# Down projections of four feed-forward stages: eight block products before, seven after

## What is computed

```python
def swiglu(h, w_gu, w_down):
    gate, up = jnp.split(h @ w_gu, 2, axis=-1)
    return (jax.nn.silu(gate) * up) @ w_down      # (256 x 2816) @ (2816 x 1024)

def sublayer(x, shift, scale, gate, g_pre, g_post, fn, res_weight):
    h = rmsnorm(x, g_pre) * (1 + scale[:, None, :]) + shift[:, None, :]
    return x + res_weight * gate[:, None, :] * rmsnorm(fn(h), g_post)
```

## Time and profile before

| | us |
|---|---|
| median of three timed runs | 2773.78 |
| lowest and highest of them | 2773.39 and 2774.01 |
| span of the profiled execution | 2775.9 |
| gate/up products of stage 0, 20 of 22 units | 138.41 |
| down products of one stage | 75.80 |
| the tail, from 1400 us to the end | 1376 |

### The profile page before, as it was taken

How to read it: one execution, slowest core, us unless ns; L and a number is a source line. 1 busy time by engine, 2 the same in 40 slices (tenths; PEclk the granted TensorE clock), 3 DMA queues, 4 the chain that set the end, 5 groups by cost and what they waited for, 6 DMA issues and landing times.

```text
span 2775.9 us, 26672 instructions
## 1 busy us (share of the span) xinstructions
PE 2463.2 (89%) x9819; PEld 1566.6 (56%) x9819; DVE 1601.6 (58%) x3550; ACT 620.1 (22%) x1778; POOL 685.0 (25%) x698
## 2 busy tenths in 40 slices
PE   7999999999999999999998877967988778877776
PEld 6874558856884678758654432634535535432222
DVE  4552144524451545513697885686887877874445
ACT  2001210001000220000143333342333533332222
POOL 1110001100110001100243443444444443444332
PEclk9999999999999999999999999989999989999999
DMA  9994427954894339957799999999999999999997
GB/s 382 383 372 165 152 95 271 361 231 152 319 363 170 144 149 380 370 202 269 293 376 421 421 422 421 413 412 421 415 421 400 421 421 415 421 392 422 421 422 326
DMA packets 120520, 931.58 MB, mean 336 GB/s; under 512 B 15133, under 2 KB 16565, under 8 KB 20422
## 3 DMA queue, kind: packets, MB, share of 16 engines
q0 software_dynamic: 94032, 670.65, 59.1%
q1 hardware_dynamic: 26358, 259.23, 23.7%
HBM read 928.74 MB, written 1.09 MB: 335 GB/s over the span
## 4 chain that ended last, share of the span: by engine, by line
PE 58%; DMA 27%; DVE 8%; ACT 3%; issue 2%; SPq 1%; POOL 1%; DVEq 0%
DMA ring<-in_peer_uv_dram,lamt 26%; PE psR L975 20%; PE psF L893 11%; PE psF L1325 10%; DVE ring L2567 3%; PE psR L863 2%; PE psR L833 2%; PE psR L822 2%; PE psR L1350 1%; POOL ring L679 1%; PE psR L1422 1%; PE psF L921 1%; PE psR L874 1%; ACT small L1765 1%; PE psF L1192 1%
## 5 line engine op out<-in xcount | busy, mean ns | idle before, releaser
L1325 PE MATMUL psF<-ring,p_diag 128*128 128x512 f32 x1792 | 868.2, 629 | 248.0 <-ACT p_diag L1771 247.7
L679 POOL DMA_INDIRECT ring<-in_peer_uv_dram,lamt x512 | 592.8, 1158 | 984.3 <-PE psF L1325 757.9
L2567 DVE SCALAR_TENSOR_TENSOR ring<-ring,h 128x1024 f32<-128x1024 f32 x512 | 620.9, 1223 | 345.5 <-DMA ring<-in_peer_uv_dram,lamt 342.4
L1325 PEld LDWEIGHTS psF<-ring,p_diag 128*128 128x128 f32 x1792 | 337.0, 198 | 709.3 <-ACT p_diag L1771 369.4
L975 PE MATMUL psR<-hT,ring 128*128 128x256 f32 x2560 | 553.3, 379 | 0.6 <-DMA ring<-in_gu_t_dram 0.6
L975 PEld LDWEIGHTS psR<-hT,ring 128*128 128x128 f32 x2560 | 486.2, 190 | 66.5 <-DMA ring<-in_gu_t_dram 0.7
L893 PE MATMUL psF<-ring,arena 128*128 128x512 f32 x704 | 303.2, 593 | 4.0 <-DVE arena L2207 4.0
L1762 ACT ACTIVATE small<-small 128x2 f32<-128x2 f32 x255 | 51.8, 203 | 825.6 <-DVE ring L2567 825.4
L893 PEld LDWEIGHTS psF<-ring,arena 128*128 128x128 f32 x704 | 133.5, 190 | 172.0 <-issue 166.4
L509 POOL DMA_DIRECT2D mring<-in_mod_t_dram x80 | 42.5, 531 | 746.3 <-DVE mring L2032 742.2
L2207 DVE TENSOR_TENSOR arena<-arena,psR 128x256 f32<-128x256 f32 x80 | 33.7, 421 | 249.7 <-ACT arena L1632 249.6
(11 more groups left out here) (341 smaller groups left out, 2289.3 us busy)
## 6 DMA issues: line engine op xcount, KB each, us to landing
ring<-in_gu_t_dram SPq DMA_DIRECT2D x44, 2048.0 KB, 9.0
mring<-in_mod_t_dram POOLq DMA_DIRECT2D x80, 1024.0 KB, 7.8
M<-in_mod_t_dram POOLq DMA_DIRECT2D x40, 1024.0 KB, 8.1
ring<-in_down_t_dram SPq DMA_DIRECT2D x20, 2048.0 KB, 9.3
mring<-in_tail_w_dram SPq DMA_DIRECT2D x40, 1024.0 KB, 9.3
ring<-in_conv_in_t_dram SPq DMA_DIRECT2D x12, 2048.0 KB, 8.1
ring<-in_gla_in_t_dram SPq DMA_DIRECT2D x6, 2048.0 KB, 7.7
ring<-in_out_t_dram SPq DMA_DIRECT2D x6, 2048.0 KB, 7.7
```

The lines of the kernel that those rows point to most:

```text
L679: pool.indirect_dma_start(out=pair(n % PAIRS), out_offset=None, in_=rows, in_offset=bass.IndirectOffsetOnAxis(ap=s_idx[:, c:c + 1], axis=0 ...
L1325: ins = pe.matmul(psF[:, b, f * HALF:(f + 1) * HALF], p_diag[:, n % PAIRS, :], row_v(n % PAIRS)[:, f * HALF:(f + 1) * HALF], start=(i == 0 ...
L2567: dve.scalar_tensor_tensor(row_u(c), row_u(c), 1.0, h[:, b, :], ALU.mult, ALU.mult, accum_out=p_dots[:, c:c + 1]).then_inc(dot_done, 1)
```

## The change

The down projection is taken as a 2 x 2 by 2 x 2 product of blocks, once for each pair p of neighbouring tiles (k = 2p, 2p + 1; eleven pairs). The left blocks are two tiles of actT by two token blocks, the right ones two weight tiles by two column halves. Instead of eight products a pair takes seven (the Strassen form with shared sums), each with a PSUM bank of its own, accumulated over all pairs.

- VectorE makes for each pair four sums of activation blocks, 128 x 128 (sum_acts), after every second gate/up unit, and four sums of weight blocks, 128 x 512 (sum_weights): pair 0 after unit 20's half steps, pair 1 after the last unit's, the others after that. The three weight sums that get their own room are double-buffered in h and hT; the sum for pair p waits for product 4 of pair p - 2 (weights_sums_used). The fourth is written over the weight tile itself.
- TensorE waits for both kinds of sum ahead of each pair (sums_ready), and no longer for the last unit before the first product. Pairs 0 to 4 take all seven products. Pairs 5 to 10 leave out products 2 and 3 (LATE_PAIRS); pairs 9 and 10 run product by product, in the order 1, 6, 7, 5, 4; then come products 2 and 3 of the six late pairs, 12 products.
- VectorE joins the seven banks into psF with eight additions or copies of 512 columns. Five can be made before product 4 is complete and one follows it (sum_products); the result for b = 0 is then whole, and ScalarE waits for that (down_summed) instead of output_done. One more, for product 2, stands between finish and prepare of b = 0, and the last, for product 3, after TensorE's last product and in front of store_modulated (sum_second).
- The stage's left-over half steps are interleaved, one behind each sum_weights; tables() stands between sum_weights 1 and 2 in stage 0.
- Down weights are stored in another order of tiles (DOWN_ORDER). Two of the preloaded chunks move one and two places later in SP's queue, because sums of activations now lie in their room.

```diff
@@ -74,9 +74,14 @@
 TURN_UNIT = (12, 15, 16, 17)
 BLOCK_KEYS_UNIT, BLOCK_SCORE_UNIT = 22, (25, 28, 31, 34)
 KEPT = {6: 5, 3: 6, 9: 7, 0: 4, 11: 8, 18: 3}
-PRELOADED = (3, 6, 9)
+PRELOADED = (6, 3, 9)
 PASSING = [(b, c) for b in range(2) for c in range(CHUNKS) if c not in KEPT]
 
+
+PAIRED = FT // 2
+LATE_PAIRS = range(5, PAIRED)
+DOWN_ORDER = [k for p in range(5) for k in (2 * p, 2 * p + 1)] + [2 * p for p in LATE_PAIRS] + [2 * p + 1 for p in LATE_PAIRS]
+ACT_SUMS = (7552, 10752, 10752, 8704)
 
 SHARED_GROUPS = range(4, 36)
...
@@ -202,7 +207,11 @@
     cb = view(6144, KD, P)
 
     actT = view(0, FT, T)
+    h_flat, hT_flat = h[:].rearrange("p b n -> p (b n)"), hT[:].rearrange("p k t -> p (k t)")
+    weight_sums = [v[:, 0:3 * HALF].rearrange("p (m n) -> p m n", m=3) for v in (h_flat, hT_flat)]
     sg = view(FT * T, 2, T)
+    sum_p1, sum_p16, sum_p167, sum_p165 = arena[:, FT * T:FT * T + HALF], hT_flat[:, 0:HALF], hT_flat[:, HALF:2 * HALF], \
+        h_flat[:, 3 * HALF:]
 
     knT = view(6144, MH, T)
     vmla = view(8192, TB, D)
...
@@ -480,6 +495,25 @@
             return psF[:, 1, (u % 3) * HALF:(u % 3 + 1) * HALF]
         return psW[u % 3][:]
 
+    def act_sum(which, m, p):
+
+        q = m * PAIRED + p
+        return arena[:, ACT_SUMS[which] + q * P:][:, 0:P] if q < 30 else macc[:, 0, (q - 30) * P:(q - 29) * P]
+
+    def down_tile(st, k):
+
+        q = DOWN_ORDER.index(k)
+        return slot(st.w + 11 + q // 4, 4, D)[:, q % 4, :]
+
+    def down_slot(k):
+        return DOWN_ORDER.index(k) // 4
+
+    def product_bank(st, product):
+
+        if product in (6, 7):
+            return psW[(st.u + 17 + product) % 3]
+        return {1: psM[:], 4: psF[:, 0, 0:HALF], 5: psF[:, 0, HALF:], 2: psF[:, 1, 0:HALF], 3: psF[:, 1, HALF:]}[product]
+
     def output_done(eng, st, b):
 
         if b == 0:
...
@@ -611,8 +645,10 @@
             load_chunk(first_chunk(n)[0], n)
 
         def load_kept(c):
-            if c in PRELOADED:
+            if c == PRELOADED[0]:
                 sp.wait_ge(x_ready, x_count(6))
+            elif c in PRELOADED:
+                sp.wait_ge(w_used, outputs[ffn3.w + LOADS["ffn"] - 1])
             elif KEPT[c] < 4:
                 sp.wait_ge(a_full, LAST_QUERY[KEPT[c] + 4] + 1)
             else:
...
@@ -639,8 +675,8 @@
                     sp.wait_ge(m_used, 2 * len(PIECES) + 2)
                     for n in range(2):
                         load_first(n)
-                if st is conv7 and j in (2, 3, 4):
-                    load_kept(PRELOADED[j - 2])
+                if st is conv7 and j in (2, 4, 5):
+                    load_kept(PRELOADED[(2, 4, 5).index(j)])
                 fill(st.w + j)
 
         for n in range(2, FIRST_CHUNKS):
...
@@ -883,33 +919,48 @@
                 u = block_by_tokens(u, w, lhs, kd, n, b)
             return u
 
-        def project(st, i, lhs, kt):
-
-            tail = 4 * ((kt - 1) // 4 - 1)
-
-            def rows_of(k, b):
-                w = slot(i + k // 4, 4, D)
-                for f in range(2):
-                    ins = pe.matmul(psF[:, b, f * HALF:(f + 1) * HALF], lhs[:, k, b * P:(b + 1) * P],
-                                    w[:, k % 4, f * HALF:(f + 1) * HALF], start=(k == 0), stop=(k == kt - 1))
-                return ins
-
-            for k in range(tail):
-                if k % 4 == 0:
-                    arrived(i + k // 4)
-                for b in range(TB):
-                    ins = rows_of(k, b)
-                if k % 4 == 3:
+        def down(st):
+
+            def product(m, p):
+
+                k, kk = 2 * p, 2 * p + 1
+                w, ww, sums = down_tile(st, k), down_tile(st, kk), weight_sums[p % 2]
+                lhs, rhs = {1: (actT[:, k, P:], w[:, 0:HALF]), 2: (actT[:, kk, P:], ww[:, 0:HALF]),
+                            3: (act_sum(st.which, 2, p), ww[:, HALF:]), 4: (actT[:, kk, 0:P], sums[:, 2, :]),
+                            5: (act_sum(st.which, 0, p), w[:, HALF:]), 6: (act_sum(st.which, 1, p), sums[:, 0, :]),
+                            7: (actT[:, k, 0:P], sums[:, 1, :])}[m]
+                return pe.matmul(product_bank(st, m), lhs, rhs, start=(p == 0), stop=(p == PAIRED - 1))
+
+            def sums_ready(p):
+                pe.wait_ge(act_summed, PAIRED * st.which + p + 1)
+                pe.wait_ge(weights_summed, PAIRED * st.which + p + 1)
+
+            for p in range(PAIRED - 2):
+                sums_ready(p)
+                for m in (1, 6, 7, 5):
+                    ins = product(m, p)
+                if p == 6:
                     ins.then_inc(w_used, 1)
-            for b in range(TB):
-                for k in range(tail, kt):
-                    if b == 0 and k % 4 == 0:
-                        arrived(i + k // 4)
-                    ins = rows_of(k, b)
-                    if b == 0 and k == kt - 1:
-                        ins.then_inc(first_ready, 1)
-                    if b == 1 and (k % 4 == 3 or k == kt - 1):
+                product(4, p).then_inc(weights_sums_used, 1)
+                if p not in LATE_PAIRS:
+                    for m in (2, 3):
+                        ins = product(m, p)
+                    if p in (1, 3):
                         ins.then_inc(w_used, 1)
+            for m in (1, 6, 7, 5, 4):
+                for p in (PAIRED - 2, PAIRED - 1):
+                    if m == 1:
+                        sums_ready(p)
+                    ins = product(m, p)
+                    if m == 4 and p == PAIRED - 2:
+                        ins.then_inc(w_used, 1)
+                ins.then_inc(first_ready if m == 4 else product_done, 1)
+            for m in (2, 3):
+                for p in LATE_PAIRS:
+                    ins = product(m, p)
+                    if m == 3 and p == 8:
+                        ins.then_inc(w_used, 1)
+                ins.then_inc(product_done if m == 2 else w_used, 1)
 
         def project_block(i, lhs, b):
...
@@ -977,8 +1028,8 @@
                                             start=(k == 0), stop=(k == KD - 1))
                     ins.then_inc(unit_full, 1)
                     u += 1
-            have(u - 1)
-            project(st, st.w + 11, actT, FT)
+            have(u - 2)
+            down(st)
 
         def gla(st):
             i = st.w
...
@@ -1983,7 +2034,10 @@
 
             for b in range(1 if st.kind == "mla" else 0, TB):
                 if st.kind not in ("kv", "conv"):
-                    output_done(act, st, b)
+                    if st.kind == "ffn":
+                        act.wait_ge(down_summed, TB * st.which + b + 1)
+                    else:
+                        output_done(act, st, b)
                     root_mean_square(st, psF[:, b, :], b)
                 if st.n < 6:
                     x_roots(stages[st.n + 1], b)
...
@@ -2206,10 +2260,79 @@
                 dve.wait_ge(gate_ready, t_gate.next())
                 dve.tensor_tensor(actT[:, j, :], sg[:, j % 2, :], ps[:, T:2 * T], ALU.mult).then_inc(unit_stored, 1)
                 u += 1
+                if j % 2 == 0:
+                    dve.wait_ge(unit_stored, u - 1)
+                    sum_acts(st, j // 2 - 1)
                 for _ in range(halves_done(st, j) - halves_done(st, j - 1)):
                     half_step()
-            while halves_taken.n < sum(2 * len(BESIDE[n]) for n in BESIDE if n <= st.n):
-                half_step()
+                if j == FT - 2:
+                    sum_weights(st, 0)
+            dve.wait_ge(unit_stored, u)
+            sum_acts(st, PAIRED - 1)
+            sum_weights(st, 1)
+            if st.n == 0:
+                tables()
+            for p in range(2, PAIRED):
+                sum_weights(st, p)
+                if halves_taken.n < sum(2 * len(BESIDE[n]) for n in BESIDE if n <= st.n):
+                    half_step()
+            sum_products(st)
+
+        def sum_acts(st, p):
+
+            k, kk = 2 * p, 2 * p + 1
+            b0, b1 = [[actT[:, t, b * P:(b + 1) * P] for t in (k, kk)] for b in range(TB)]
+            s1, s2, s4 = [act_sum(st.which, m, p) for m in range(3)]
+            link(dve.tensor_tensor(s1, b0[0], b0[1], ALU.add))
+            dve.tensor_tensor(b0[0], b1[0], b0[0], ALU.subtract)
+            link(dve.tensor_tensor(s2, s1, b1[0], ALU.subtract))
+            dve.tensor_tensor(s4, b1[1], s2, ALU.subtract).then_inc(act_summed, 1)
+
+        def sum_weights(st, p):
+
+            k, kk = 2 * p, 2 * p + 1
+            w, ww = down_tile(st, k), down_tile(st, kk)
+            if p >= 2:
+                dve.wait_ge(weights_sums_used, (PAIRED - 2) * st.which + p - 1)
+            for i in sorted({down_slot(k), down_slot(kk)}):
+                dve.wait_ge(w_loaded[home_of(st.w + 11 + i)], landed[st.w + 11 + i])
+            t2, t3, t4 = [weight_sums[p % 2][:, m, :] for m in range(3)]
+            b11, b12, b21, b22 = w[:, 0:HALF], w[:, HALF:], ww[:, 0:HALF], ww[:, HALF:]
+            dve.tensor_tensor(t3, b22, b12, ALU.subtract)
```

(48 more changed lines are left out.)

## The result

| | before | after |
|---|---|---|
| median of the runs, us | 2773.90 (4 runs) | 2755.82 (4 runs) |
| lowest and highest | 2773.39 and 2778.68 | 2749.45 and 2755.93 |
| span of the profiled execution | 2775.9 | 2747.7 |

The ratio is 0.9924, with a 95% interval from 0.991 to 0.9938: 18.1 us less in the medians. The profiled execution is the one of 2749.45 us; the three others lie within 0.2 us of 2755.8. That gap of 6.4 us is the main thing to explain, since the forecast was 2750.8. Wherever both are given, the device time stands 1.7 to 1.8 us above the span. So the profiled execution of the kernel before took some 2777.7 us, an estimate, and was 3.8 us longer than the median, where its span alone shows 2.0.

What follows compares the result with a forecast made beforehand. TensorE was taken to bound the stages that change. Products saved less gaps, clock and boundaries leave 6.8 us each in stages 2, 4, 6 and 2.6 in stage 0: 2773.8 - 23.0 = 2750.8 us, range 2745 to 2761.

Steps and rivals of the forecast that it cites:

- rival A: Down projections: the clock also falls at the four gaps of 2.16 us, 6.8 us, giving 2757.6; chance 0.12.
- Rival B: TensorE's many short gaps in the four stages together lower its clock; about 2773 us, no change; chance 0.05.
- Rival D: The front ends earlier but the tail, with its full DMA, ends when it did; 2773.8 us; chance 0.04.
- gap behind the tables: Stage 0: tables() between weight sums 1 and 2 takes 5.8 us and leaves TensorE 2.5 us idle.
- gap at pair 8: Stage 0: weight sum 8 is ready at 48.1 us but wanted at 47.0, so TensorE idles 1.1 us.
- gap ahead of pair 10: Each down projection: sum_weights 10 waits for product 4 of pair 8, so TensorE idles 2.16 us.
- Products: Down projections: seven products instead of eight per pair, 0.861 us each, save 9.5 us per stage, 37.9 us in all.
- Prices of sums: VectorE: sum_weights 2.76 us and sum_acts 1.16 us per pair; PSUM sums at SBUF's price, or 0.75 us as other end.
- Boundary: End of each stage: the 12-product cover for b = 0 holds, L2086 starts later; 0.2 us lost per stage.
- Moved DMA loads, half steps: Later preloaded chunks and loads costed at nothing; no half step's DMA wait over a microsecond in the down projections.
- Rival C: Down projections: half steps' DMA waits now stand in front of TensorE, 73 us slower, 2823 us; chance 0.04.
- Clock: Half clock only behind stage 0's 2.5 us gap, 1.7 us with 0.6 left; the 2.16 us gaps at full clock.

Runs made afterwards that it cites:

- e1: The changed kernel run again without any edit: median 2757.59 us in six runs, ratio 0.9926 to the kernel before.
- e3: Changed kernel with TensorE starting each pair on products that need no weight sum, reading tiles as loaded: 2736.64 us, ratio 0.9855 to the kernel before.
- e7: Kernel before with only the two preloaded chunks moved later in SyncE's queue: 2775.74 us, ratio 1.0.
- e5: Changed kernel with one useless VectorE sum more in front of sum_weights 10 in each stage: 2759.45 us, ratio 0.9936 to the kernel before.
- e6: Changed kernel with the weight buffer given back one product earlier (order 6, 7, 1, 4, 5): 2747.64 us, ratio 0.9898 to the kernel before.
- e2: Changed kernel with the weight buffer given back two products earlier (order 6, 7, 4, 1, 5): 2743.65 us, ratio 0.9882 to the kernel before.
- e4: e3 with VectorE's stage 0 work reordered, tables() behind weight sum 2 and left-over half steps later: 2732.80 us, ratio 0.9845 to the kernel before.

## Why the prediction was right, and where it was not

The forecast was 2750.8 us in a range from 2745 to 2761. Measured were 2755.8 and, with six more runs, 2757.6 us. Inside the range, right in sign and size, but the usual time is that of rival A (2757.6), which had a chance of 0.12, and the forecast's own is the rarer one: 2749.45 and 2750.88, two runs of ten.

That the forecast's 23.0 us meets the 23.4 us between the first two profiles is in part luck: 1.6 us of these are the GLA stage's clock, and the fall that was priced at 0.6 us in stage 0 did not come there, while one that wasn't counted cost 1.7 us in stage 6. With the clock left out on both sides, 23.0 + 0.6 = 23.6 us stand against 21.8 + 1.7 = 23.5 us. So the products, the idle gaps and the boundaries were right by more than luck, and the clock was not. The chances don't quite fit each other either: rivals B and D, 0.05 and 0.04, both mean no change, but "within it" has 0.06.

Point by point, losses in us; gaps are taken between starts, and the rows of gaps are those of the first profile of the changed kernel:

| step | forecast | stage 0 | stage 2 | stage 4 | stage 6 |
|---|---|---|---|---|---|
| first product after the last unit's end | 0.45 | 0.38 | 0.38 | 0.38 | 0.38 |
| gap at pair 1 | 0.9 | 0.82 | 1.19 | 0.82 | 0.82 |
| gap behind the tables | 2.5 | 2.40 | | | |
| gap at pair 8 | 1.1 | 0.82 | 0 | 0 | 0 |
| gap ahead of pair 10 | 2.16 | 2.23 | 2.23 | 2.23 | 2.23 |
| fall of the clock, first profile | 0.6 in stage 0 | 0 | 0 | 0 | 1.7 |
| fall of the clock, e1 | | 1.7 + 1.7 | 1.7 | 1.7 | 1.7 |

- **Products**: 0.861 us forecast, 0.860 measured (e3). Right.
- **Prices of sums**: the weight sums took 0.684 to 0.692 us and the pair's four 0.61, 0.72, 0.72 and 0.69 us from start to start, as in the trace above; the lower and upper ends of the forecast (no cost of a wait, 0.75 us) are both off. Sums that write into PSUM, which had no row, took 0.70 us:

```profile
L2302 DVE TENSOR_TENSOR ring<-ring 128x512 f32<-128x512 f32 x44 | 30.1, 684 | 0.0
...
L2324 DVE TENSOR_TENSOR psF<-psF,hT 128x512 f32<-128x512 f32 x4 | 2.8, 700 | 1.2 <-PE psF L932 1.2
```

- **On the Trainium skill's sentence** that a semaphore between VectorE instructions costs nothing extra ("VectorE: DVE Perf Modes", the DRAIN you can't avoid): here a sum without a wait behind it hands over after 0.61 us (238.57 to 239.18), one with a wait after 0.72 (239.18 to 239.90). The measurement differs from the page, and it was right to keep the rows.
- **Boundary**: 0.2 us forecast. In stage 0 the last join stands where it was put, 0.20 us behind the first transpose, and store_modulated (L2086 before, L2140 now) begins 0.81 us behind the transpose instead of 0.72: 0.1 us. The 12-product cover for b = 0 held.

```profile
259.56 1.04 PE L822 MATMUL psR<-ident,h 128*128 128x128 f32 x8
...
259.76 0.70 DVE L2335 TENSOR_TENSOR psF<-psF,h 128x512 f32<-128x512 f32 x1 [1.15 <-PE psF L932]
...
260.37 2.63 DVE L2140 TENSOR_SCALAR hT<-psR,small 128x128 f32<-128x128 f32 x8
```

- **Moved DMA loads, half steps**: nothing, as forecast (e7). The half steps wait less than before, not more: the page's group of them (L2032 before, L2086 after) had 13.4 us of idle time, 13.3 of it for DMA, and has 1.1. Rival C did not come.

```profile
L2032 DVE SCALAR_TENSOR_TENSOR mring<-mring,M 128x1024 f32<-128x1024 f32 x96 | 113.6, 1220 | 13.4 <-DMA mring<-in_mod_t_dram 13.3
```

```profile
L2086 DVE SCALAR_TENSOR_TENSOR mring<-mring,M 128x1024 f32<-128x1024 f32 x96 | 113.5, 1220 | 1.1 <-DMA mring<-in_mod_t_dram 1.1
```

- **Clock**: the step that failed. "The 2.16 us gaps I count at full clock" rested on one row of the tail, 2.24 us of gap and full speed behind it. One instance says that a gap of this length may pass; it doesn't say that it does. And that trace had others. Behind a gap of 2.54 us, longer than that, four records took 1.98 us; behind one of 2.18 us, shorter, they took 3.49:

```profile
2190.67 1.98 PE L1325 MATMUL psF<-ring,p_diag 128*128 128x512 f32 x4 [2.54 <-ACT p_diag L1771]
...
2202.04 3.49 PE L1325 MATMUL psF<-ring,p_diag 128*128 128x512 f32 x4 [2.18 <-ACT p_diag L1771]
```

So both outcomes were on record before the forecast, and the term should have had a chance, not a nothing. In the two profiles of the changed kernel 5 of the 8 gaps of 2.23 us had a fall behind them; at 2.84 us it was 4 of 4 (e5), at 1.37 us 0 of 4 (e6). In e1 each of the four down projections pays 1.7 us, 6.8 us together. The first profile pays it once, so 5.1 us of the step from 2749.5 to the usual time can be these falls; that it is made of them is inferred from e1, e2, e5 and e6, since no execution at 2755.8 us was profiled. That stage 0's fall costs less than 1.7 us because VectorE's lateness at pair 8 swallows a part was right: in e1 that gap is gone.
- **Rival B** (many short gaps together): no. The time isn't 2773 us. In the first profile stages 0, 2 and 4 have all their gaps and a granted clock of 1.00 throughout, and so it is in all four down projections of e6.
- **Rival D** (the tail takes the gain back): no. Every kernel's tail was between 1531.7 and 1536.6 us, while the front moved by 41.

Put together, with the front of e1: 1239.4 - 1222.9 = 16.5 us of gain, and the medians say 18.1 and 18.3; the rest, 1.7 us, is within what two tails of one kernel differ by. TensorE's way in e1: 37.9 us of products removed, less 12.5 us of gaps (16.5 us by the table without pair 8's 0.82, which is gone in e1, less the 4.0 us of the earlier trace rows), less 8.5 us for five falls, less 0.4 us at the boundaries, is 16.5 us. That it meets to the tenth is chance: it leaves out 0.7 us by which this execution reached its first down projection early. In e4 the same sum is 37.9 + 4.0 - 1.0 = 40.9 us, and its front stands 41.3 us earlier; the 43.1 us of the medians are within the tail's scatter of that.

What stays open: why a 2.23 us gap has a fall behind it in one execution and none in another. The same gap, in the same place, did both. Nor does the slow stretch begin at the same distance behind it: in stage 6 of the first profile the first product behind the gap was slow (2.05 us for its two records), in e1 the first was at or near full pace behind all four (1.10 to 1.16 us) and the next ones slow. So the moment at which a gap falls is a candidate, but no experiment here separates it from anything else that varies between executions. And the counts are small, one profiled execution for each length but 2.23 and 2.40 us.

## What to carry to other kernels

When work is taken from the bound engine and given to a neighbour, lay the neighbour's schedule along the stage and look at the places where a double buffer must come round between two consecutive items: here one such place, ahead of pair 10, cost 8.9 us of idling in the four stages and 1.7 to 6.8 us for the clock behind it, out of 37.9 us saved. Before adding buffers, order the consumer's work so that what frees the buffer comes first and what needs nothing new comes last; moving one product two places (e2) was worth 13.9 us. And price a gap of TensorE twice, once as idle time and once for the clock behind it. For the second, look at every gap of about that length in the profile, not at one; where some have half clock behind them and some don't, give it a chance.

## What the runs showed that I had not expected

A gap's price in these down projections is not a fixed number. In the profiles 0.5 and 1.4 us of gap cost themselves, 2.8 us cost itself and 1.7 us more at every one of four places, and 2.2 us did one or the other. The changed kernel's first four runs stand at two times 6.4 us apart. Making the gap 0.86 us shorter (e1 to e6) gave 10.0 us for 3.4 us of idling; making it 0.61 us longer (e5) cost 1.9 us.

The Trainium skill advises against idle gaps of TensorE between bursts of matmuls because its clock falls back ("TensorE: Matmul & The Clock Gate", in its table on why this matters for your kernels). The gaps that it names there are longer than these. The traces here agree that the clock falls, from 2.4 to 1.2 GHz, and show it behind gaps of 2.2 to 2.8 us already, in the windows of e1 and e5 above.
